# Latent attention with positions on partitions: squares summed along rows, operands turned by TensorE

## What is computed

```python
c_q = rms_norm(h @ w_q_a, q_a_norm)                       # 384 latent features
q = (c_q @ w_q_b).reshape(1, 512, 16, 64 + 32)
q_nope = rms_norm(q[..., :64], q_nope_norm)
q_rope = apply_rope(rms_norm(q[..., 64:], q_rope_norm), cos, sin)
c_kv = rms_norm(ckv[..., :256], kv_a_norm)                # 256 latent features
k_rope = apply_rope(rms_norm(ckv[..., 256:], k_rope_norm), cos, sin)   # shared by all heads
kv = (c_kv @ w_kv_b).reshape(1, 512, 16, 64 + 64)
k_nope, v = rms_norm(kv[..., :64], k_nope_norm), kv[..., 64:]
```

## Time and profile before

| | us |
|---|---|
| median of 3 runs (1800.91 to 1801.32) | 1800.92 |
| the profiled execution | 1800.97 |
| its span, first to last instruction | 1799.2 |
| TensorE busy over the span | 1755.8 (98%) |
| VectorE, ScalarE, GpSimd busy | 1234.6, 931.8, 488.0 |

### The profile page before, as it was taken

How to read it: one execution, slowest core, us unless ns; L and a number is a source line. 1 busy time by engine, 2 the same in 40 slices (tenths; PEclk the granted TensorE clock), 3 DMA queues, 4 the chain that set the end, 5 groups by cost and what they waited for, 6 DMA issues and landing times.

```text
span 1799.2 us, 27385 instructions
## 1 busy us (share of the span) xinstructions
PE 1755.8 (98%) x10262; PEld 1417.5 (79%) x10262; DVE 1234.6 (69%) x1863; ACT 931.8 (52%) x1668; POOL 488.0 (27%) x383
## 2 busy tenths in 40 slices
PE   9999999999999999999999999999999999999997
PEld 6778799999887656678999988778666777866675
DVE  8964488887446677758888835465676576567657
ACT  6634466654224677646566522232567633366763
POOL 0870267674000000006776600122000213200010
PEclk9999999999999999999999999999999999999999
DMA  6322322323333111122323233333111133312111
GB/s 217 91 90 82 94 95 95 118 95 118 95 97 95 40 32 29 59 82 72 117 95 118 93 117 89 96 96 97 59 59 48 48 93 100 101 47 59 49 60 56
DMA packets 58799, 152.64 MB, mean 85 GB/s; under 512 B 17024, under 2 KB 22048, under 8 KB 58672
## 3 DMA queue, kind: packets, MB, share of 16 engines
q1 hardware_dynamic: 55120, 148.24, 26.5%
q0 software_dynamic: 3552, 2.70, 0.6%
HBM read 143.76 MB, written 4.19 MB: 82 GB/s over the span
## 4 chain that ended last, share of the span: by engine, by line
PE 84%; DVE 6%; ACT 4%; POOL 3%; issue 2%; DMA 0%; SPq 0%; ACTq 0%; DVEq 0%; POOLq 0%
PE bank L2420 11%; PE bank L2421 11%; PE bank L2422 11%; PE bank L2633 8%; PE bank L2635 7%; PE bank L2634 7%; PE bank L2989 3%; PE bank L2991 3%; PE bank L2990 3%; PE bank L2942 2%; PE bank L2971 2%; PE bank L2972 2%; PE bank L2973 2%; PE bank L2713 1%; DVE wl L1532 1%
## 5 line engine op out<-in xcount | busy, mean ns | idle before, releaser
L1532 DVE TENSOR_TENSOR wl<-raw,wh 128x1024 fp32r<-128x1024 f32 (+3 forms) x199 | 234.1, 1176 | 271.3 <-ACT wh L831 266.9
L831 ACT ACTIVATE wh<-raw 128x1024 fp32r<-128x1024 f32 (+3 forms) x199 | 193.0, 970 | 354.1 <-PE bank L2422 287.6
L2420 PE MATMUL bank<-hidH,wh 128*128 128x512 f32 x352 | 137.4, 390 | 0.0
L2421 PE MATMUL bank<-hidL,wh 128*128 128x512 f32 x352 | 137.0, 389 | 0.0
L2422 PE MATMUL bank<-hidH,wl 128*128 128x512 f32 x352 | 136.9, 389 | 0.0
L2633 PE MATMUL bank<-xH,wh 128*128 128x256 f32 x480 | 135.8, 283 | 0.0
L2634 PE MATMUL bank<-xL,wh 128*128 128x256 f32 x480 | 135.8, 283 | 0.0
L2635 PE MATMUL bank<-xH,wl 128*128 128x256 f32 x480 | 135.8, 283 | 0.0
L2989 PE MATMUL bank<-xH,wh 128*128 128x512 f32 x256 | 111.3, 435 | 5.9 <-ACT qk L1395 3.1
L742 POOL TENSOR_TENSOR raw<-raw,wsum 128x512 f32<-128x512 f32 x40 | 86.6, 2164 | 110.9 <-DVE wl L1861 110.9
L2991 PE MATMUL bank<-xH,wl 128*128 128x512 f32 x256 | 100.8, 394 | 0.0
(11 more groups left out here) (522 smaller groups left out, 5210.8 us busy)
## 6 DMA issues: line engine op xcount, KB each, us to landing
raw<-w_gu_dram SPq DMA_DIRECT2D x88, 512.0 KB, 3.7
raw<-w_p_dram SPq DMA_DIRECT2D x64, 512.0 KB, 3.6
raw<-w_dn_dram SPq DMA_DIRECT2D x32, 448.0 KB, 3.4
raw<-w_glu_dram SPq DMA_DIRECT2D x16, 512.0 KB, 3.6
raw<-w_dn_dram SPq DMA_DIRECT2D x16, 512.0 KB, 3.7
raw<-w_out_dram SPq DMA_DIRECT2D x16, 512.0 KB, 3.5
raw<-w_in_dram SPq DMA_DIRECT2D x8, 512.0 KB, 7.7
raw<-w_o_dram SPq DMA_DIRECT2D x8, 512.0 KB, 3.6
```

Of the source, the lines that this page charges most:

```text
L831: nc.scalar.activation(wh[:, (st.base + u) % 2, 0:kts * P], raw[:, (st.base + u) % 4, 0:kts * P], ACT.Copy).then_inc(w_high, 1)
L1532: nc.vector.tensor_tensor(wl[:, s, 0:kts * P], raw[:, (st.base + u) % 4, 0:kts * P], wh[:, s, 0:kts * P].bitcast(F32), ALU.subtract).then_ ...
L2420: nc.tensor.matmul(bank, wh[:, s, w], hi[:, k, :], start=first and kt == 0, stop=False)
L2421: nc.tensor.matmul(bank, wh[:, s, w], lo[:, k, :], start=False, stop=False)
```

## The change

Queries and keys are now made with positions on partitions. A **unit** is one tile of 128 positions of one part: `("n", g)` the nope columns of four heads (256 wide), `("r", g)` the rope columns of eight heads (256 wide, no turned copy in the weights), `("k", g)` the nope keys of eight heads (512 wide). There are 32 units, in the order of `UNITS`; now the latent is the loaded operand and the weights move. A unit is nine matmuls of 256 columns, or six of 512 for keys. ScalarE squares it, VectorE sums the squares along the row in groups (`unit_sums`), ScalarE takes the inverse root of the 4 or 8 sums (`root_of_unit`, two instructions), and VectorE multiplies the bank by the roots into `q_rows` or `k_rows` (`scale_unit`; for rope three instructions, two of which write the turned copy). `turn_queries` and `turn_keys` then turn a head's queries or a pair's keys by four transposes into bank 7; VectorE multiplies the queries by the rope and gain table into `qst` (`take_queries`), and ScalarE copies the keys with their gain into `kst` (`take_keys`, two instructions of 64x512). Twelve units stand ahead of the loop with four banks, two more between the first scores, and 18 inside heads 0 to 9: 3, 3, 2, 2, 2, 2, 1, 1, 1, 1. Weight blocks of 384 and 256 columns (24 of them) become eight of 768 or 1024; the two of the values stay. The `qtab` tables are made earlier, between the latents of stage `a`. In the first stretch ScalarE runs `unit_square(n)` and `root_of_unit(n - 1)` in turn and then the value copies and `take_keys`.

```diff
-BLOCKS_B = [("q", 0), ("k", 0), ("v", 0), ("v", 1), ("q", 1), ("k", 1)]
-for _p in range(1, NH // 2):
-    BLOCKS_B += [("q", 2 * _p), ("q", 2 * _p + 1)] + [("k", _p + 1)] * (_p + 1 < NH // 2)
+BLOCKS_B = [("q", 0), ("q", 1), ("k", 0), ("v", 0), ("v", 1), ("q", 2), ("q", 3), ("k", 1), ("q", 4), ("q", 5)]
 AT_B = {kind: n for n, kind in enumerate(BLOCKS_B)}
+WIDE = {"q": 4 * DN, "k": 8 * DN, "v": S}
...
+UNITS = [(part, t) for part in (("n", 0), ("r", 0), ("k", 0), ("n", 1), ("r", 1), ("k", 1), ("n", 2), ("n", 3)) for t in range(QT)]
...
+UNITS_EARLY = 3 * QT + 2
+UNITS_IN = {}
...
+for _h, _n in enumerate((3, 3, 2, 2, 2, 2, 1, 1, 1, 1)):
...
+    def unit_part(n):
+        (kind, _), _ = UNITS[n]
+        o = banks[(2, 3, 4, 5)[n % 4] if n < 3 * QT else 2 + n % 2]
+        return o[:, 0:WIDE["k" if kind == "k" else "q"]]
...
+            def unit_square(n):
+                part, t = UNITS[n]
+                act.wait_ge(sem("unit_made"), n + 1)
+                if t == QT - 1:
+                    act.sem_inc(w_used, 1)
+                o = unit_part(n)
+                nc.scalar.activation(unit_squares[n % 2][:, 0:o.shape[1]], o, ACT.Square).then_inc(sem("unit_squared"), 1)
+
+            def root_of_unit(n):
+                part, t = UNITS[n]
+                groups = 4 if part[0] == "n" else 8
+                act.wait_ge(sem("unit_summed"), n + 1)
+                inverse_root(unit_root[:, n % 2, 0:groups], unit_sum[:, n % 2, 0:groups], 1.0 / (DR if part[0] == "r" else DN), sem("unit_rooted"))
...
+            def take_keys(pair):
+                act.wait_ge(sem("k_turned"), pair + 1)
+                for s, rows in enumerate((slice(0, DN), slice(DN, P))):
+                    nc.scalar.activation(kst[pair % 2][s][rows, :], banks[7][rows, :], ACT.Identity,
+                                         scale=vecs[rows, VEC["k_head"]:VEC["k_head"] + 1]).then_inc(sem("kv_used"), 1)
...
             for h in range(NH):
                 pair, s = h // 2, h % 2
-                if h + 2 < NH:
-                    query_squares(h + 2)
-                    if h + 2 < NH - 2:
-                        ahead(st, 0, AT_B["q", h + 2], True)
+                units = UNITS_IN.get(h, [])
                 for j in range(QT):
                     if j < 3:
                         copy_turned(h, j)
                     if h + 1 < NH:
                         probs(h + 1, 1 - s, j)
-                    if j == 1 and h + 2 < NH:
-                        query_root(h + 2)
-                        if s and pair + 2 < NH // 2:
-                            key_squares(pair + 2)
-                            ahead(st, 0, AT_B["k", pair + 2], True)
-                    if j == 2 and s and pair + 2 < NH // 2:
-                        key_root(pair + 2)
+                    if 1 <= j <= len(units):
+                        root_of_unit(units[j - 1])
+                        ahead_of_unit(units[j - 1])
+                    if j < len(units):
+                        unit_square(units[j])
+                if s and pair + 2 < NH // 2:
+                    take_keys(pair + 2)
                 if pair and s == 0:
                     output_high(pair - 1)
-                if NH - 2 <= h + 2 < NH:
-                    ahead(st, 0, AT_B["q", h + 2], True)
...
+            def unit_sums(n):
+                part, t = UNITS[n]
+                groups = 4 if part[0] == "n" else 8
+                dve.wait_ge(sem("unit_squared"), n + 1)
+                nc.vector.tensor_reduce(unit_sum[:, n % 2, 0:groups], unit_groups(n, unit_squares[n % 2][:, 0:unit_part(n).shape[1]]), AX, ALU.add)\
+                  .then_inc(sem("unit_summed"), 1)
+
+            def scale_unit(n):
+                (kind, g), t = UNITS[n]
+                dve.wait_ge(sem("unit_rooted"), n + 1)
+                pairs = 2 if kind == "n" else 4
+                root = unit_root[:, n % 2, 0:2 * pairs].rearrange("p (q s) -> p q s", s=2).unsqueeze(3)
+                o = unit_part(n).rearrange("p (q s d) -> p q s d", q=pairs, s=2)
+                if kind == "n":
+                    at = g % 2 * 2
+                    copies = [(q_rows[g // 2][:, at:at + 2, t, 0:4:3, :], o)]
+                elif kind == "k":
+                    copies = [(k_rows[g][:, :, t, :, :], o)]
+                else:
+                    to, half = q_rows[g][:, :, t, 1:3, :], DR // 2
+                    copies = [(to[:, :, :, 0:DR], o), (to[:, :, :, DR:DR + half], o[:, :, :, half:DR]), (to[:, :, :, DR + half:DN], o[:, :, :, 0:half])]
+                for to, of in copies:
+                    nc.vector.tensor_tensor(to, of, root.to_broadcast(list(of.shape)), ALU.mult).then_inc(sem("unit_scaled"), 1)
...
+                dve.wait_ge(sem("q_turned"), h + 1)
+                nc.vector.tensor_tensor(qst[s][:, :], banks[7][:, :], qtab[s][:, :], ALU.mult).then_inc(sem("qk_ready"), 1)
...
+            unit_sums(0)
+            for n in range(1, 3 * QT):
+                unit_sums(n)
+                if n == 4:
+                    ahead(st, 0, 0, True)
+                scale_unit(n - 1)
+                if n == 5:
+                    normalise(range(5, 6))
+                    nc.vector.tensor_tensor(T[:, 3, :], latent(5), ropeT[:, :], ALU.mult).then_inc(sem("krope_part"), 1)
+                if n == 8:
+                    ahead(st, 0, 1, True)
+                if n == 9:
+                    dve.wait_ge(sem("krope_folded"), 1)
+                    rope_rows(0)
...
+                units = UNITS_IN.get(h, [])
+                share_first(h)
+                for n in to_scale:
+                    scale_unit(n)
...
                 if pair and s:
                     output_low(pair - 1)
-                if s == 0 and 1 <= pair < NH // 2 - 1:
-                    head_keys(pair + 1)
                 if h + 2 < NH:
-                    head_queries(h + 2)
-                if s and pair + 2 < NH // 2:
-                    ahead(st, 0, AT_B["k", pair + 2], True)
+                    take_queries(h + 2)
+                for n in units[1:2]:
+                    scale_unit(n - 1)
+                    ahead_of_unit(n - 1)
+                    unit_sums(n)
...
+            def unit(n):
+                part, t = UNITS[n]
...
+                wide, rows = o.shape[1], slice(t * P, (t + 1) * P)
+                hi, lo, kts = (cvH, cvL, KKV) if part[0] == "k" else (cqH, cqL, KQ)
+                if t == 0:
+                    pe.wait_ge(w_split, b + 5)
+                before = n - 4 if n < 3 * QT + 2 else n - 2
+                if before >= 0:
+                    pe.wait_ge(sem("unit_scaled"), SCALED[before])
+                for kt in range(kts):
+                    w = slice(kt * wide, (kt + 1) * wide)
+                    nc.tensor.matmul(o, hi[:, kt, rows], wh[:, b % 2, w], start=kt == 0, stop=False)
+                    nc.tensor.matmul(o, hi[:, kt, rows], wl[:, b % 2, w], start=False, stop=False)
+                    ins = nc.tensor.matmul(o, lo[:, kt, rows], wh[:, b % 2, w], start=False, stop=kt == kts - 1)
+                ins.then_inc(sem("unit_made"), 1)
+
+            def turn_queries(h):
+                pair, s = h // 2, h % 2
+                pe.wait_ge(sem("unit_scaled"), SCALED[AT_U[("r", h // 8), QT - 1]] if h < 4 else max(SCALED[AT_U[part, QT - 1]] for part in (("r", h // 8), ("n", h // 4))))
                 if h:
-                    pe.wait_ge(sem("rq_ready"), h)
-                    pe.wait_ge(sem("rk_ready"), min(h // 2 + 1, NH // 2))
+                    pe.wait_ge(sem("qk_ready"), h)
+                    pe.wait_ge(sem("kv_used"), 3 if h == 1 else 1 + 2 * min(NH // 2, 2 + (h - 2) // 2))
                 else:
                     pe.wait_ge(sem("latroot_ready"), 3)
-                nc.tensor.matmul(banks[7][:, :], mean_of("mean_odd" if h % 2 else "mean_even"), T[:, 0, :], start=True, stop=True)\
-                  .then_inc(sem("qstat_ready"), 1)
-
-            def key_mean(pair):
-                pe.wait_ge(sem("ksq_ready"), pair + 1)
-                pe.wait_ge(sem("rq_ready"), max(2 * pair, 1))
-                nc.tensor.matmul(banks[7][:, :], mean_of("mean_pair"), T[:, 2, :], start=True, stop=True)\
-                  .then_inc(sem("kstat_ready"), 1)
+                for t in range(QT):
+                    ins = nc.tensor.transpose(banks[7][:, t * P:(t + 1) * P],
+                                              q_rows[h // 8][:, pair % 4, t, 2 * s:2 * s + 2, :].rearrange("p a b -> p (a b)"), const("ident"))
+                ins.then_inc(sem("q_turned"), 1)
+
+            def turn_keys(pair):
+                pe.wait_ge(sem("unit_scaled"), SCALED[AT_U[("k", pair // 4), QT - 1]])
+                pe.wait_ge(sem("qk_ready"), 1 + pair if pair < 2 else 2 * pair)
+                if pair:
+                    pe.wait_ge(sem("kv_used"), 2 * pair + 1)
+                for t in range(QT):
+                    ins = nc.tensor.transpose(banks[7][:, t * P:(t + 1) * P],
```

(46 more changed lines are left out.)

201 lines of the change are left out of this document (99 added, 102 removed).

## The result

The changed kernel takes 1830.93 us, median of 4 runs (1830.81 to 1831.95). The kernel before takes 1800.91 (1800.52 to 1801.32). The ratio is 1.0168, with a 95% interval of 1.0150 to 1.0186: slower by 30.0 us. The forecast was 1807.5, with a range to 1817. The sign was right, the size less than a quarter of what came.

The account below looks back on a forecast made before the run. TensorE was taken to bound the stage (19.6 of 20 us busy), VectorE and ScalarE three quarters full. First stretch +13.3, loop -6.3 and head 14 -0.4 gave +6.6 on 1800.97: forecast 1807.5, range 1794 to 1817.

Parts of the forecast that it names:

- TensorE's work: Whole stage: narrower query products and transposes in place of means cut TensorE's own work from 69.7 to 49.6 us.
- First stretch, +13.3: Ahead of the loop over heads: VectorE's work and the bank 7 ladder make it 41.5 us instead of 28.2.
- The ladder over bank 7: End of first stretch: queries and keys take turns in one bank, so the first scores come only near 632.1.
- Rival 2: First stretch not held by VectorE: TensorE alone takes 35.0 instead of 41.5, total 1801.0, about no change; 20%.
- Key copies: Ahead of heads 2, 4, ... 12: the queries' turning waits for ScalarE's two key copies, 0.69 us each.
- Rival 1: Ahead of heads 2 to 12: copies do not hold TensorE up, six gaps of 2.5 go, 1792.5; 16%.
- The loop, -6.3: Heads 0 to 13: 124.5 us instead of 130.8, with hand-over gaps in even heads and VectorE-bound odd ones.
- So TensorE turns queries at 2.95 after the scores: Even-head hand-over: minimum, exponential and two key copies follow the last scores; TensorE uses 0.44 us and idles 2.5.
- the odd heads VectorE-bound: Odd heads of the loop: VectorE's work, not TensorE's 1.35 + 3.70, sets 5.7 us without units.
- minus 0.4: Behind the loop: head 14's first product loses its wait of 0.42 us.
- less than 1.00 anywhere from 600 to 770: Sign on the granted clock in the stage: if it shows this, rival 3 holds.
- rival 3: Clock falls in the six even-head gaps, 1 to 3.7 us each: 1813 to 1830, about 1818; 14%.

Follow-up runs that it names:

- e4_first_order: The changed kernel with first values stored ahead of the last roots and queries 0 and 1 taken ahead of VectorE's splits: 1830.86 us.
- g_order: All the changed kernel's work in another order on TensorE, ScalarE and VectorE, no product added: 1803.21 us.
- e2_fill: The changed kernel with unread products put in TensorE's gaps, order and work of the rest unchanged: 1819.45 us.

## Why the prediction was wrong

**TensorE's work** came as counted: nine matmuls of 256 columns 1.1, four transposes 0.44. That the gain would be eaten was right, and so was where.

**First stretch, +13.3.** 41.5 forecast, 43.6 measured, 42.0 at full clock. The ladder over bank 7 and VectorE's strict order held; the root of a unit is shown by ScalarE at 604.79:

```profile
604.79 0.30 ACT L889 ACTIVATE unit_root<-unit_sum,tiny 128x4 f32<-128x4 f32 x1 [1.08 <-DVE unit_sum L2073]
605.12 0.21 ACT L890 ACTIVATE unit_root<-unit_root 128x4 f32<-128x4 f32 x1
```

It ends 0.54 after its start (0.45 taken). VectorE was through with the twelve units and the third split at 625.7 (625.3 forecast), and the first scores came at 634.2 for 632.1: in between VectorE idled 5.8 us, for a split that stands late in ScalarE's order. Rival 2 is out, but VectorE's total was not the whole reason: e4_first_order and g_order shortened the stretch to 41.0 and 38.3 with the same work.

**Key copies.** 0.69 each forecast, 1.38 a pair measured, and in four of the six even heads they are the releaser that was named. In heads 6 and 10 the last to come was the scaling of a unit that the queries of heads 8 and 12 need, which the forecast had overlooked. Rival 1 is out.

**The loop, -6.3.** This is the term that failed: it was +14.5. Of the 20.8 between them, the step "minimum 694.44 to 695.13 ... So TensorE turns queries at 2.95 after the scores" gave the even heads a gap of 2.5. It assumed VectorE free when the last scores end, as the rows of the kernel before show it. There the TensorE-bound pass left VectorE idle at that point. In the faster odd head VectorE is the late one, by 0.5 without units and more with them; I had called the odd heads VectorE-bound and yet started the next chain with an idle VectorE. Ahead of heads 2, 4 and 6 ScalarE's root and split (1.3) stand in the chain as well; I had counted them for head 2 alone. At full clock (e2_fill) the loop is 134.4, 9.9 over the forecast: 3.3 in heads 0 and 1, 7.7 in the even heads, -1.1 in the odd. Of the 7.7, 7.0 is in the six hand-overs: 19.0 was forecast for them (2.95 each, 1.3 more ahead of head 2), and e2_fill took 26.0. How that divides between VectorE's late minima, ScalarE's roots and splits and the scaling of the last unit is read from the rows; no run singled it out. The "minus 0.4" behind this term was counted twice: the 130.8 of the old loop already holds that wait.

**The clock** took the other 10.9. By the prediction's own sign ("less than 1.00 anywhere from 600 to 770") rival 3 holds. It had 14% as an alternative, "against it: the gap is shorter than that". The gaps ahead of the even heads were longer than the 2.5 forecast, 3.0 to 4.5. But it was never an alternative to the forecast; it comes on top of it, and 1807.5 with its 11.5 and the longer chains' 9.9 gives 1828.9. The last 2 are small terms that e2_fill still holds: the first product 0.7 later, 0.5 in the first stretch, the 0.4 counted twice, 0.4 behind the loop. That rival 3's own range, 1813 to 1830, ends within a microsecond of the result is luck: it had six falls and no late VectorE. By the rule of the Trainium skill (TensorE: Matmul & The Clock Gate, Part 1) an idle TensorE falls to half clock and earns the full one back by sustained work: the trace agrees, with 0.66 in the window behind head 8's gap of 3.02, 0.60 to 0.72 around head 6's, and 11.5 us less when the gaps are filled; behind head 10's gap of 3.30 it shows no fall. The second rule, that transposes don't count as busy, no run here singled out.

**Range and chances.** Each case was priced alone, and two that come together (longer gaps, and the clock behind them) were not put together. With the sizes measured since, the clock alone makes 1819 and both make 1829; the upper end belonged there.

## What to carry to other kernels

When a change frees the engine that was the bound, time the chain behind it with the other engines' queues as they will stand then; the idle moments that the old trace shows in them were made by the old bound. A wait that a trace names is the last of its chain: before moving one step, list what each engine has in front of the next three, and move them together; here single moves gained 0 to 3.5 us, all of them 27.7. And gaps of a few us on TensorE can be paid twice, as seven of the eight of 2.4 to 4.5 us in this loop were, so price gap and clock as one case; unread products in the gaps measure the second part.

## What the runs showed of the hardware

- Here the clock fell in the gap or behind it: near 717.2 in head 6, 2.3 us before work resumed, and at 741.0 in head 8, 1.3 us after. The length of the gap alone does not decide: 3.02 ahead of heads 8 and 12 led to 0.66 in a 5-us window, 3.30 ahead of head 10 to 1.00 throughout.
- It was down behind shorter gaps too: 0.75 from 660 to 665, behind head 1's 2.40; 0.66 from 625 to 630, behind 2.21 in the first stretch; 0.50 from 700 to 705 in g_order, where TensorE had waited 1.19 and then 1.75. The same loop had 0.91 in one kernel and 0.88 in another (e4_first_order), 2.6 us apart.
- Very short ScalarE steps are cheap but not free: 0.30 for a Ln over 4 columns, against 0.69 over 512.
